# The recurrence's chunked scan in fewer, wider products: 128x128 head products, doubling with a shared side, one bank per product

## What is computed

```python
def step(state, inp):
    r_t, w_t, k_t, v_t, kk_t, a_t = inp
    sa = jnp.einsum('dbhij,dbhj->dbhi', state, -kk_t)
    state = (state * w_t[..., None, :] + sa[..., :, None] * (kk_t * a_t)[..., None, :]
             + v_t[..., :, None] * k_t[..., None, :])
    return state, jnp.einsum('dbhij,dbhj->dbhi', state, r_t)

_, ys = lax.scan(step, state0, inputs)
y = (ys[:, 0] + jnp.flip(ys[:, 1], 0)).transpose(1, 0, 2, 3)
```

## Time and profile before

| what | before |
|---|---|
| median of 3 runs | 3576.79 us |
| the profiled execution | 3584.42 us |
| its span, first to last instruction | 3583.1 us |
| its mean granted TensorE clock | 0.976 |
| TensorE busy | 3295.2 us, 92% |
| DVE, ACT, POOL busy | 1607.3, 1094.6, 332.8 us |
| instructions | 52220 |

### The profile page before, as it was taken

The page is one execution under the profiler, slowest core; times in us unless marked ns, Lnnn a source line. Parts: engine busy times, 40 slices in busy tenths (PEclk is TensorE's granted clock), DMA queues, the critical chain, the costliest instruction groups (busy, mean ns, idle before and its releaser), DMA issues.

```text
span 3583.1 us, 52220 instructions
## 1 busy us (share of the span) xinstructions
PE 3295.2 (92%) x22912; PEld 2500.4 (70%) x22912; DVE 1607.3 (45%) x2207; ACT 1094.6 (31%) x1692; POOL 332.8 (9%) x382
## 2 busy tenths in 40 slices
PE   8999999999999999999999999757768999888887
PEld 6888787888887888896788887557745887423223
DVE  4443547544336443327544336853476444201102
ACT  3222226432224222226422233444324323100001
POOL 1000122100000000001100002131141001000001
PEclk9999999999999999999999999879989999999998
DMA  3223320122232222332122223000010223699996
GB/s 134 94 86 97 121 83 25 60 94 94 89 99 100 96 101 87 106 118 83 60 95 105 85 92 107 30 32 4 4 71 27 81 100 112 247 428 423 427 425 254
DMA packets 58258, 445.86 MB, mean 124 GB/s; under 512 B 6960, under 2 KB 8112, under 8 KB 28080
## 3 DMA queue, kind: packets, MB, share of 16 engines
q1 hardware_dynamic: 58032, 442.53, 33.4%
HBM read 440.40 MB, written 2.10 MB: 123 GB/s over the span
## 4 chain that ended last, share of the span: by engine, by line
PE 81%; DMA 7%; DVE 7%; ACT 2%; issue 2%; POOL 0%; SPq 0%; DVEq 0%; POOLq 0%; ACTq 0%
PE bank L165 21%; PE bank L166 21%; PE bank L167 20%; PE bank L2204 5%; DMA xe<-in_exp_up 3%; PE bank L1607 3%; DMA xe<-in_exp_gate 3%; PE bank L1599 2%; PE bank L782 2%; PE bank L749 2%; PE bank L765 2%; DMA xe<-in_exp_down 2%; PE bank L2280 1%; PE bank L662 1%; DVE w_lo L482 1%
## 5 line engine op out<-in xcount | busy, mean ns | idle before, releaser
L482 DVE TENSOR_TENSOR w_lo<-slot,w_hi 128x2048 fp32r<-128x2048 f32 (+4 forms) x243 | 489.3, 2014 | 332.9 <-ACT w_hi L473 331.6
L165 PE MATMUL bank<-xa,w_hi 128*128 128x512 f32 x1368 | 546.8, 400 | 21.7 <-DVE xa L525 9.9
L166 PE MATMUL bank<-xa,w_hi 128*128 128x512 f32 x1368 | 535.3, 391 | 0.0
L167 PE MATMUL bank<-xa,w_lo 128*128 128x512 f32 x1368 | 535.0, 391 | 0.0
L473 ACT ACTIVATE w_hi<-slot 128x2048 fp32r<-128x2048 f32 (+4 forms) x243 | 405.7, 1670 | 383.8 <-PE bank L167 383.1
L165 PE MATMUL bank<-xb,w_hi 128*128 128x512 f32 x832 | 327.0, 393 | 9.0 <-DVE w_lo L482 9.0
L166 PE MATMUL bank<-xb,w_hi 128*128 128x512 f32 x832 | 325.1, 391 | 0.0
L167 PE MATMUL bank<-xb,w_lo 128*128 128x512 f32 x832 | 325.0, 391 | 0.0
L165 PEld LDWEIGHTS bank<-xa,w_hi 128*128 128x128 f32 x1368 | 258.4, 189 | 83.5 <-issue 11.1
L166 PEld LDWEIGHTS bank<-xa,w_hi 128*128 128x128 f32 x1368 | 258.3, 189 | 59.2 <-issue 6.5
L167 PEld LDWEIGHTS bank<-xa,w_lo 128*128 128x128 f32 x1368 | 258.3, 189 | 53.9
(11 more groups left out here) (418 smaller groups left out, 5126.1 us busy)
## 6 DMA issues: line engine op xcount, KB each, us to landing
slot<-in_w_gu SPq DMA_DIRECT2D x87, 1024.0 KB, 4.9
slot<-in_exp_gate SPq DMA_DIRECT2D x24, 2048.0 KB, 13.5
slot<-in_exp_up SPq DMA_DIRECT2D x24, 2048.0 KB, 15.8
slot<-in_exp_down SPq DMA_DIRECT2D x24, 2048.0 KB, 15.8
slot<-in_w_dn SPq DMA_DIRECT2D x64, 704.0 KB, 4.0
slot<-in_w_gate SPq DMA_DIRECT2D x24, 768.0 KB, 4.3
xe<-in_exp_gate SPq DMA_DIRECT2D x8, 2048.0 KB, 14.6
xe<-in_exp_up SPq DMA_DIRECT2D x8, 2048.0 KB, 15.9
```

The lines of the kernel that those rows point to most:

```text
L165: e.matmul(out, w[0], x[0], start=(j == 0), stop=False)
L166: e.matmul(out, w[0], x[1], start=False, stop=False)
L167: return e.matmul(out, w[1], x[0], start=False, stop=(j == n - 1))
L482: dve.e.tensor_tensor(lo, slot(k, b), hi.bitcast(F32), ALU.subtract).then_inc(L.up("w_lo", b))
```

## The change

One chunk's work is written anew, with 12 steps and a lag of 6.

- **Layout.** Heads lie by direction: direction d has partitions 64d to 64d+63 of every intermediate tile, all 8 heads side by side in 512 columns. AL and RT become one buffer (ALRT), BT and KT another (BTKT, key kinds side by side within each chunk and pair).
- **Head.** One matmul with 128 columns of keys as weights and 128 columns of queries (AL and RT) replaces four: 16 of these per chunk (two row halves, a bank per direction and x) give N, M, Ib and Ik. NT stays a 16-matmul product over four corners.
- **Doubling.** Q is multiplied through: Q1 = I + D, Q2 adds Y2 Q1, Q3 adds Y4 Q2, Q adds Y8 Q3. Y2 times (Q1 next to X2) is one product of 128 columns.
- **Second level.** Z, then G = I + Z, and two products with only the 32 and the 16 late columns (G2, G3).
- **Stacked sources.** U and vT lie in one tile (UV), bT and kT in another (bkT), so that y and S need one product each over 128 partitions; vT and bkT are made by 16 transposes of 128x128. The state's own part of y is a product of its own (y1), in step 8.
- **Banks.** `product` (16 matmuls over two corners) writes one bank, and one instruction empties it.

Per chunk, 480 matmuls become 320 and 16 transposes. The core of the diff:

```diff
@@ plan_memory
-    m.first, m.second = [b.buf(512, f"first{i}_") for i in range(8)], [b.buf(512, f"second{i}_") for i in range(4)]
-    m.kept = [{n: b.buf(512, n) for n in ("M", "Ib", "Ik", "bT", "kT", "vT")} for _ in range(2)]
+    m.NM, m.BK_in = ([[b.buf(512, n) for _ in range(2)] for _ in range(2)] for n in ("NM", "IbIk"))
+    m.QX = [b.buf(1024, "QX").rearrange("p (z c) -> p z c", z=2) for _ in range(2)]
+    m.DT, m.offT, m.Y, m.ZT, m.G, m.V1 = (b.buf(512, n) for n in ("DT_W", "offT", "Y2_Y8", "Y4_ZT", "G", "QtW"))
+    m.MV = b.buf(512, "MtvT")
+    m.UV, m.bkT = ([b.buf(512, n) for _ in range(2)] for n in ("UV", "bkT"))
...
-    m.AL, m.RT, m.BT, m.KT = ([b.buf(2048, n) for _ in range(2)] for n in ("AL", "RT", "BT", "KTL"))
+    m.ALRT = b.buf(8192, "ALRT").rearrange("p (z d c) -> p z d c", z=2, d=2)
+    m.AL, m.RT = ([m.ALRT[:, z, d, :] for d in range(2)] for z in range(2))
+    m.BK = b.buf(8192, "BTKT").rearrange("p (d j c x) -> p d j c x", d=2, j=4, c=8)
+    m.BT, m.KT = ([[m.BK[:, d, j, :, (z ^ d) * 64:(z ^ d) * 64 + 64] for j in range(4)] for d in range(2)] for z in range(2))
@@ chunk_turns
-LAG = 7
-STEPS = 13
+LAG = 6
+STEPS = 12
 HALVES = (slice(0, 64), slice(64, 128))
+HEADS = [(d, j, x) for j in range(4) for x in range(2) for d in range(2)]
@@ pe_scan
+    def product(name, i, freed, lhs, rhs, n=64):
+        bank = bank_for(name, i, 0, freed)
+        for d, j, x in HEADS:
+            c = (2 * j + x) * n
+            last = e.matmul(bank[HALVES[d], c:c + n], lhs(d, j, x), rhs(d, j, x), start=True, stop=True)
+        last.then_inc(L.up(S, name, i))
...
+        def state(d, j, x):
+            return m.state[HALVES[x], (4 * d + j) * 64:(4 * d + j) * 64 + 64]
+
         if s == 0:
-            turn("N", i, (V, "off"), (bt, al))
-            turn("NT", i, (V, "DT"), (al, bt))
+            for d in range(2):
+                banks = [bank_for("head", i, (d, x), (V, "I", i, d, x)) for x in range(2)]
+                for j in range(4):
+                    for x in range(2):
+                        last = e.matmul(banks[x][:, j * P:(j + 1) * P], to_keys(d, j)[HALVES[x]], to_queries(d, j, x),
+                                        start=True, stop=True)
+                last.then_inc(L.up(S, "head", i, d))
+            banks = [bank_for("NT", i, x, (V, "offT", i, x)) for x in range(2)]
+            for d, j, x in HEADS:
+                last = e.matmul(banks[x][HALVES[d], j * 64:j * 64 + 64], to_queries(d, j, x, 0), to_keys(d, j, 0)[HALVES[x]],
+                                start=True, stop=True)
+            last.then_inc(L.up(S, "NT", i))
...
+            product("Y4", i, (A, "Y4", i), X, Y2)
+            pe.wait_ge(*L.at(C, "Q1", i, 1))
+            banks = [bank_for("Q2", i, b, (V, "Q2", i, 1) if b else (A, "X4", i, 0)) for b in range(2)]
+            for d, j, x in HEADS:
+                h = 2 * j + x
+                last = e.matmul(banks[h // 4][HALVES[d], h % 4 * P:h % 4 * P + P], Y2(d, j, x), QX[HALVES[d], :, h * 64:h * 64 + 64],
+                                start=True, stop=True)
...
+            product("G2", i, (V, "G2", i, 1), ZT, lambda d, j, x: late(m.G, d, 32)[:, 2 * j + x, :], 32)
+            for d in range(2):
+                bank = bank_for("vT", i, d, (A, "vT", i, d))
+                for j in range(4):
+                    c = 64 * d + j * 512 + here[d].start
+                    last = e.transpose(bank[:, j * P:(j + 1) * P], m.V_edged[:, c:c + P], k.ident)
+                last.then_inc(L.up(S, "vT", i, d))
+            for d in range(2):
+                bank = bank_for("bkT", i, d, (A, "bkT", i, d))
+                for j in range(4):
+                    last = e.transpose(bank[:, j * P:(j + 1) * P], to_keys(d, j), k.ident)
...
+            product("V1", i, (A, "V1", i), Q, DT)
...
+            product("U", i, (A, "U", i, 1), G, own(m.V1))
...
+            bank = bank_for("S", i, 0, ("state_sum", i))
+            for d, j, x in HEADS:
+                c = (4 * d + j) * 64
+                last = e.matmul(bank[HALVES[x], c:c + 64], head_of(m.bkT[d], j, x), head_of(m.UV[d], j, x), start=True, stop=True)
+            last.then_inc(L.up(S, "S", i))
+            bank = bank_for("y", i, 0, ("y_added", i, 1))
+            for d, j, x in HEADS:
+                c = (4 * d + j) * 64
+                last = e.matmul(bank[HALVES[x], c:c + 64], head_of(m.UV[d], j, x), head_of(BK_in[d], j, x), start=True, stop=True)
+            last.then_inc(L.up(S, "y", i))
@@ dve_scan
+            for d in range(2):
+                dve.wait_ge(*L.at(S, "head", i, d))
+                for x in range(2):
+                    e.tensor_tensor(quad_to(NM[d], x), head(d, x, 0), mask(d, 4), ALU.mult).then_inc(L.up(V, "D", i, d, x))
+            dve.wait_ge(*L.at(S, "NT", i))
+            for name, dst, z in (("DT", m.DT, 4), ("offT", m.offT, 5)):
+                for x in range(2):
+                    e.tensor_tensor(quad_to(dst, x), quad(k.banks.of("NT", i, x)), mask(z, 4), ALU.mult).then_inc(L.up(V, name, i, x))
+            for d in range(2):
+                for x in range(2):
+                    e.tensor_tensor(quad_to(BK_in[d], x), head(d, x, 1), mask(2 + d, 4), ALU.mult).then_inc(L.up(V, "I", i, d, x))
...
+        if s == 11:
+            dve.wait_ge(*L.at(S, "y", i))
+            e.tensor_tensor(ST, k.banks.of("S", i, 0)[:, :], ST, ALU.add).then_inc(L.up("state_sum", i))
+            dve.wait_ge(*L.at("state_sum", i))
             for d in range(2):
                 c = chunk_at(d, i)
                 half = f4(ST[:, d * 256:(d + 1) * 256])
                 e.tensor_tensor(half, half, m.ptc[d][:, :, c:c + 1].to_broadcast([P, 4, 64]), ALU.mult).then_inc(L.up("state", i, d))
+            dve.wait_ge(*L.at("y_begun", i, 1))
```

More of the change, by code:

```diff
@@ L1634, in pe_scan @@
[L1634 to L1645 removed]
+            pe.wait_ge(*L.at(A, "X2", i))
@@ new lines, in pe_scan @@
+        if s == 7:
+            pe.wait_ge(*L.at(V, "G2", i, 1))
+            product("G3", i, (V, "G3", i, 1), ZT, lambda d, j, x: late(m.G, d, 16)[:, 2 * j + x, :], 16)
+            pe.wait_ge(*L.at(A, "vT", i, 1))
+            product("MV", i, (A, "MV", i), lambda d, j, x: head_of(NM[d], j, x)[HALVES[1 - d]],
+                    lambda d, j, x: head_of(m.UV[d], j, x)[HALVES[1 - d]])
+        if s == 8:
+            pe.wait_ge(*(L.at("state", i - 1, 1) if i else L.at("state_clear")))
+            banks = [bank_for("W", i, x, (V, "W", i, x)) for x in range(2)]
+            for d, j, x in HEADS:
+                last = e.matmul(banks[x][HALVES[d], j * 64:j * 64 + 64], to_queries(d, j, x, 0), state(d, j, x), start=True, stop=True)
+            last.then_inc(L.up(S, "W", i))
+            bank = bank_for("y1", i, 0, ("y_begun", i, 1))
+            for d, j, x in HEADS:
+                c = (4 * d + j) * 64
+                last = e.matmul(bank[HALVES[x], c:c + 64], state(d, j, x), to_queries(d, j, x, 1), start=True, stop=True)
+            last.then_inc(L.up(S, "y1", i))
@@ L1731, in act_scan @@
+        if s == 2:
+            whole("Y4", i, m.ZT)
+            act.wait_ge(*L.at(S, "Q2", i))
+            for b in (1, 0):
+                if b == 0:
+                    act.wait_ge(*L.at("chunk_vector", "Q2", i, 0))
+                e.activation(X[:, b * 256:(b + 1) * 256].rearrange("p (h t) -> p h t", h=4),
+                             k.banks.of("Q2", i, b).rearrange("p (h t) -> p h t", h=4)[:, :, 64:128], ACT.Copy).then_inc(
+                    L.up(A, "X4", i, b))
         if s == 3:
-            act.wait_ge(*L.at(C, "IY2", i))
@@ new lines, in act_scan @@
+        if s == 6:
+            for d in range(2):
+                h = HALVES[1 - d]
+                act.wait_ge(*L.at(S, "vT", i, d))
+                e.activation(m.UV[d][h, :], k.banks.of("vT", i, d)[h, :], ACT.Copy).then_inc(L.up(A, "vT", i, d))
+            for d in range(2):
+                act.wait_ge(*L.at(S, "bkT", i, d))
+                e.activation(m.bkT[d], k.banks.of("bkT", i, d)[:, :], ACT.Copy).then_inc(L.up(A, "bkT", i, d))
+        if s == 7:
+            whole("MV", i, m.MV)
@@ L1747, in act_scan @@
+        if s == 8 and i < 4:
+            act.wait_ge(*L.at(S, "y1", i))
+            for d in range(2):
+                c = chunk_at(d, i) * 64
+                e.activation(f4(k.y_rwkv)[:, :, c:c + 64], f4(k.banks.of("y1", i, 0)[:, d * 256:(d + 1) * 256]), ACT.Copy).then_inc(
+                    L.up("y_copied", i, d, also=[("y_begun", i, d)]))
         if s == 9:
-            act.wait_ge(*L.at(S, "R1", i))
-            turn("P", i, g[0])
+            whole("V1", i, m.V1)
         if s == 10:
-            turn("W", i, g[2])
@@ L1752, in act_scan @@
-        if s == 11:
-            act.wait_ge(*L.at(S, "P", i))
-            turn("U", i, g[1])
-        if s == 12 and i < 4:
-            act.wait_ge(*L.at(S, "y", i))
-            for x in range(2):
-                for d in range(2):
-                    c = chunk_at(d, i) * 64
```

(15 more changed lines are left out.)

328 lines of the change are left out of this document (125 added, 203 removed).

## The result

The changed kernel takes 3558.24 us (median of 4 runs, 3552.8 to 3565.03). On the same chip the kernel before takes 3578.1 us (4 runs, 3576.72 to 3580.03). The ratio is 0.9936, with a 95% interval of 0.9913 to 0.9959. That is 19.9 us less, where 22.9 were forecast, and 3558 lies in the predicted range of 3540 to 3571.

The account below looks back on a forecast made before the run. Recurrence bound by arrival of its own instructions. Fill 44, six periods 150, last chunk 19, y and S 1.9, to yc 3.7: 218.6 us against 241.5, 22.9 less; median 3576.8 to 3554, 8-in-10 range 3540 to 3571.

Parts of the forecast that it names:

- The period: Steady part, from one chunk's S to the next: 25 us, from work 20.7, waits and changes of form; 28.65 before.
- Waits: TensorE's idle time per steady period: 1.4 before G2, 1.1 X2, 0.35 Y8, 0.2 Q, 0.5 S.
- X2: Doubling product in step 7, waiting for the bank of the first head product: starts at 12.5 us, 1.1 late.
- changes of form: Switches between 64-row and 128-row products, five a period, each costing TensorE a tail, taken as 0.15 us.
- columns in proportion: Pricing rule for TensorE products: time scales with columns, giving G2 0.5, G3 0.4 and head 1.8 us.
- Fill: Start of the recurrence, chunk 0 alone first, 7.3 us of it at 1.2 GHz: 44 us, against 40.2 before.
- last chunk: Final chunk alone, its waits bare: 16 us, and 3 more for a clock at 1.2 GHz.
- tail: End of the scan: VectorE adds state before y, then the sum over y: 3.7 us to yc, after y and S 1.9.
- Rival 1: Two-corner products: row halves writing one bank alternate, each costing double; 56 us slower, 3633 us; chance 8%.
- Rival 2: Scan: pauses are not instruction arrival, or evictions lose more; period 28 to 29, 3570 to 3580 us; chance 10%.
- Rival 3: Scan: fewer waits than counted, PE-bound; period 21 us, 55 us less, 3522 us; chance 8%.
- Edits priced at nothing: Wider-step reading of BT and KT, two more edge memsets, smaller masks: hidden in idle time, under 1 us if uncovered.

Follow-up runs that it names:

- run 1: Kernel before with half of every four-corner product left out, fewer instructions at the same TensorE time: period 22.35 us instead of 28.65; one run 3549.69 us.
- run 11: Repeat of run 1 on a second chip: period 22.34 to 22.43 us, recurrence 196.8 us, one run of 3534.01 us.
- Run 2: Kernel before with a lag of 8 turns between chunks instead of 7: period 30.2 us in the mean, recurrence 252.5 us, one run 3603.1 us.
- run 5: Changed kernel with G2 and G3 over all 64 columns instead of 32 and 16: period 24.22 us against 24.19.
- run 3: Changed kernel again, unaltered, with more rounds (the second comparison): 3557.7 us against 3577.73 for the kernel before, ratio 0.9942; recurrence 210.8 us.
- run 10: Changed kernel again, unaltered, on another chip (the third comparison): 3559.32 us against 3586.28 for the kernel before, ratio 0.9937; scan 214.0 us.
- run 4: Changed kernel with step 6's 16 transposes moved ahead of G2: 3552.12 us, ratio 0.992 to the kernel before; period 23.20 us.
- run 8: Run 7's kernel with the second half of U's eviction copied by VectorE instead of ACT: 3545.27 us, ratio 0.9869; period 22.92 to 23.03 us.
- run 7: Changed kernel with transposes before G2 and without the last chunk's unread state: 3544.49 us, ratio 0.9872 to the kernel before; period 23.20 us.

## Why the prediction came out right, and where its terms were off

**The bound.** "The recurrence is bound by the arrival of its own instructions" is what runs 1 and 11 show (28.65 to 22.35 us per chunk by fewer instructions alone), with the pauses 254 instructions apart in the trace of before; the trace after shows its other side: packets 4.7 us apart in the mean and no pause inside a product. Run 2 adds what the prediction left out: the chain was close behind.

**The period.** 25 was forecast, 24.19 measured; two errors stand against each other.
- Waits: 3.55 forecast, some 2.3 measured. G2 1.09 (1.4), X2 0.31 (1.1), Y8 0.31 (0.35), Q 0.12 (0.2), S 0.42 (0.5). X2 is the one that was mis-sized, though its start was not (12.67 us after S, forecast 12.5): TensorE came to it later than reckoned, because the products in front took longer.
- Work and changes of form: 21.45 forecast, 21.9 measured. Too low were G2 (1.05 for 0.5), G3 (0.86 for 0.4) and head (1.98 for 1.8): "columns in proportion" fails below 64 columns (run 5). Too high were the transposes (1.90 for 2.04) and the changes of form: five of 0.15 would be 0.75 us, but what shows beyond 0.93 to 0.98 is 0.1 behind y (1.08), and as much behind G2 (1.08 with all 64 columns in run 5).

So the price of a narrow product was mis-sized by 1.0 us for G2 and G3 together, and the wait for X2 behind them was 0.8 shorter than forecast, which hid most of it.

**Fill, last chunk, tail.** The fill (44, measured 43.4) held; it was 42.7 in run 3 and 46.6 in run 10. The last chunk was priced at 16 and 3 for a lower clock; it took 15.75 at full clock, and the clock fell only behind it, in the last turn (0.76), and in run 10 not at all. Such a fall was read from one execution, and in runs 4 and 8 the last chunk took 15.4 to 15.8, but 16.88 in run 7. The tail was 3.7 from y's end, measured 3.4; S and y before it, forecast 1.9, took 3.6, most of it at the lower clock. The forecast had the loss of clock, but too large and one stretch too early.

**The whole.** The trace gives 29.2 us for the recurrence, where 22.9 were forecast: the six steady chunks took 3.9 us less than forecast, the last chunk 3.2 and the fill 0.6, the last turn 1.4 more. The medians give 19.9, 20.0 and 27.0 us in three comparisons. That the first is within 3 us of the forecast is in part luck. Two of the four executions after had a mean clock of 0.974 (3562.83 and 3565.03 us), and by their times none of the four before did. The lower two after, 3552.8 and 3553.65, are 25 us below the median before; sorted by mean clock in the same way, the second comparison gives 20 and 22 us and the third 25 and 25. The scan varies less, 240.2 and 241.5 us before and 210.8, 212.3 and 214.0 after, a gain of 26 to 31. So some microseconds of what the scan gives don't reach the whole, and no run here shows where they go; that stays open.

**The rivals.** Rival 1 (row halves in one bank take turns) is refuted: 32 records over two corners take 0.93 to 0.98 us, not 1.9. The Trainium skill (TensorEngine Tiling (Array Packing), Gotcha 1: PSUM Pressure) says that different row tiles cannot access one bank simultaneously; this trace doesn't agree where they write different partitions of it. Rival 2 (no instruction bound) is refuted by runs 1 and 11. Rival 3 (21 us a period, TensorE-bound) didn't come, but runs 4 and 8 go towards it: with the order of G2 and U's eviction changed, the period falls to 22.9, with 21.9 of work.

**Edits priced at nothing.** The wider writes of BT and KT show in no time: the first product starts at 2357.10 instead of 2357.32 us, and between 2354 and 2357 us in every other trace of either kind.

**A better version.** Runs 4, 7 and 8 beat both kernels. At a mean clock of 0.976 to 0.978 the kernel after took 3552 to 3556 us, runs 4 and 7 3544 to 3547, and run 8 3539 to 3545.

## What to carry over

Where TensorE idles behind "issue" in the middle of a product, with no semaphore there, count the instruction packets in that stretch, and the instructions between two pauses: if the packets are evenly spaced without a break and each pause comes one packet of instructions behind the last, fewer and wider matmuls gain even where TensorE's own time doesn't fall. Then work out the new chain turn by turn, and look at what stands in front of the eviction it waits for: here the additions to state and y ahead of G left TensorE idle for a microsecond per chunk, and moving products that wait for nothing into that gap gave it back. Price a 64x64 product narrower than 64 columns like one of 64.
